# A fused two-layer decoder trunk: the last expert's end regrouped (picked rows, spread, last norm, branch order)

## The reference, cut to what matters

```
logits = xt @ w_router
top_v, top_i = top_k(logits, 2)
gates = softmax of the two, scattered to 8 experts
for e in range(8):
    h = xt @ w_gu[e]                                  # (256, 1024) @ (1024, 5632)
    y = (silu(h[:, :2816]) * h[:, 2816:]) @ w_down[e]
    out = out + gates[:, e] * y
x = layer_norm(alpha * x + out, g, b)                 # fp32, mean and variance over 1024
```

## Time and profile before

| | |
|---|---|
| median of 3 runs | 1303.49 us (1302.29 to 1306.15) |
| the profiled execution | 1302.73 us, of it the span 1300.9 us |
| TensorE busy | 1257.2 us (97%) |
| VectorE busy | 989.1 us (76%) |
| ScalarE busy | 823.9 us (63%) |
| GpSimd busy | 95.7 us (7%) |
| moved by transfers | 375.80 MB, mean 289 GB/s |

### The profile page before, as it was taken

The page is one execution under the profiler, slowest core; times in us unless marked ns, Lnnn a source line. Parts: engine busy times, 40 slices in busy tenths (PEclk is TensorE's granted clock), DMA queues, the critical chain, the costliest instruction groups (busy, mean ns, idle before and its releaser), DMA issues.

```text
span 1300.9 us, 17514 instructions
## 1 busy us (share of the span) xinstructions
PE 1257.2 (97%) x7133; PEld 1092.7 (84%) x7133; DVE 989.1 (76%) x827; ACT 823.9 (63%) x820; POOL 95.7 (7%) x116
## 2 busy tenths in 40 slices
PE   8999999999999979999999999999999999999994
PEld 8997987999988967888888888888888888888883
DVE  6876844554445575788888888888898988898896
ACT  5794343434434464577777777777777777778772
POOL 4043210200000100300000000000000000001000
PEclk9999998999999999999999999999999999999997
DMA  9743011997554522699999999999999999999990
GB/s 317 256 146 130 1 34 65 384 371 249 188 188 144 193 65 98 218 384 406 389 385 400 383 388 375 388 384 375 386 388 372 390 379 383 384 386 362 388 395 38
DMA packets 188854, 375.80 MB, mean 289 GB/s; under 512 B 12240, under 2 KB 69696, under 8 KB 188768
## 3 DMA queue, kind: packets, MB, share of 16 engines
q1 hardware_dynamic: 179744, 345.02, 73.3%
q0 software_dynamic: 6864, 25.81, 5.2%
q10 hardware_dynamic: 2160, 3.79, 0.8%
HBM read 354.12 MB, written 20.45 MB: 288 GB/s over the span
## 4 chain that ended last, share of the span: by engine, by line
PE 87%; DVE 5%; ACT 4%; DMA 2%; issue 1%; POOL 1%; SPq 1%; DVEq 0%; ACTq 0%
PE ps L1394 84%; PE ps L1791 1%; DMA raw<-in_moe_w_gu 1%; DVE lo L901 1%; DVE conv L982 1%; ACT hi L546 1%; DMA raw<-in_dn_w_in 1%; ACT sS L750 1%; PE ps L1784 0%; SPq L293 0%; DVE x L1360 0%; ACT ps L561 0%; ACT ps L599 0%; PE ps L1692 0%; ACT zn L599 0%
## 5 line engine op out<-in xcount | busy, mean ns | idle before, releaser
L901 DVE TENSOR_TENSOR lo<-raw,hi 128x2048 fp32r<-128x2048 f32 x326 | 744.8, 2297 | 173.6 <-ACT hi L546 172.7
L546 ACT ACTIVATE hi<-raw 128x2048 fp32r<-128x2048 f32 x326 | 625.4, 1919 | 317.1 <-PE ps L1394 287.3
L1394 PE MATMUL ps<-hi,xg_hi 128*128 128x512 f32 x704 | 277.5, 394 | 0.4 <-DVE lo L901 0.4
L1394 PE MATMUL ps<-hi,xg_lo 128*128 128x512 f32 x704 | 274.5, 390 | 0.0
L1394 PE MATMUL ps<-lo,xg_hi 128*128 128x512 f32 x704 | 274.1, 389 | 0.0
L1394 PE MATMUL ps<-xT_hi,hi 128*128 128x256 f32 x624 | 177.6, 285 | 2.1 <-DVE xT_lo L909 2.1
L1394 PE MATMUL ps<-xT_lo,hi 128*128 128x256 f32 x624 | 176.5, 283 | 0.0
L1394 PE MATMUL ps<-xT_hi,lo 128*128 128x256 f32 x624 | 176.5, 283 | 0.0
L1394 PEld LDWEIGHTS ps<-hi,xg_hi 128*128 128x128 f32 x704 | 132.2, 188 | 28.2 <-DVE lo L901 1.2
L1394 PEld LDWEIGHTS ps<-hi,xg_lo 128*128 128x128 f32 x704 | 132.1, 188 | 28.0
L1394 PEld LDWEIGHTS ps<-lo,xg_hi 128*128 128x128 f32 x704 | 132.3, 188 | 26.4
(11 more groups left out here) (293 smaller groups left out, 1266.5 us busy)
## 6 DMA issues: line engine op xcount, KB each, us to landing
raw<-in_moe_w_gu SPq DMA_DIRECT2D x352, 512.0 KB, 7.3
raw<-in_moe_w_down SPq DMA_DIRECT2D x176, 512.0 KB, 6.7
raw<-in_ffn_w_gu SPq DMA_DIRECT2D x44, 512.0 KB, 8.3
raw<-in_dn_w_in SPq DMA_DIRECT2D x32, 512.0 KB, 9.0
raw<-in_ffn_w_down SPq DMA_DIRECT2D x22, 512.0 KB, 4.0
xe<-xTf POOLq DMA_DIRECT2D x1, 8192.0 KB, 29.0
raw<-in_dn_w_out SPq DMA_DIRECT2D x8, 512.0 KB, 3.9
ys<-xTf POOLq DMA_DIRECT2D x1, 4096.0 KB, 40.1
```

The source lines that it names most:

```text
L546: act.activation(slot(hi, j), slot(raw, j), ACT.Copy).then_inc(hi_ready, 1)
L901: dve.tensor_tensor(slot(lo, j), slot(raw, j), slot(hi, j).bitcast(F32), ALU.subtract).then_inc(lo_ready, 1)
L1394: return pe.matmul(dst, lhsT, rhs, start=start, stop=stop)
```

## The change

Picked rows: the two rows of block 0 are added at units 26 and 28 of the last expert, the two of block 1 at unit 30. The spread goes half by half (columns 0 to 511 of both blocks, then the rest), with a signal for each of the four, and VectorE adds it in four operations of 512 columns with a sum each; `whole_sum` adds a block's two sums. The norm of block 0 begins (mean) ahead of block 1's second half. TensorE runs nine fillers behind the last unit, and the five ahead of the first expert are gone. SyncE branches first and waits for the stores behind the branch.

```
+        lnhalf = sb("lnhalf", [P, NB, 2])
...
-            sp_.wait_ge(out_done, 16 * NB)
             with sp_.If(full > P):
+                sp_.wait_ge(out_done, 16 * NB)
                 experts(1)
                 store(4)
                 sp_.wait_ge(out_done, 32 * NB)
+            sp_.wait_ge(out_done, 16 * NB)
...
-            def norm(i, bank, last=None):
+            def norm(i, bank, last=None, summed=None, between=None):
...
-                    mean(0)
-                    mean(1)
+                    for b in range(NB):
+                        if b and between:
+                            between()
+                        if summed:
+                            summed(b)
+                        mean(b)
                     centre(0)
                     centre(1)
                     finish(0)
...
+                            if p == 0 and last and b == 1 and l in (GU_E + 4, GU_E + 6):
+                                add_picked(0, (l - GU_E - 4) // 2)
                             if p == 0 and last and b == 1 and l == PER_E - 3:
-                                for n_ in range(2 * NB):
-                                    add_picked(n_ // 2, n_ % 2)
+                                add_picked(1, 0)
+                                add_picked(1, 1)
...
-            for b in range(NB):
-                dve.wait_ge(spread, b + 1)
-                dve.scalar_tensor_tensor(out=x[:, b, :], in0=ps[:, 2 * b:2 * b + 2, :].rearrange("p i n -> p (i n)"),
-                                         scalar=g7[:, b, :], in1=x[:, b, :], op0=ALU.mult, op1=ALU.add,
-                                         accum_out=lnsum[:, b:b + 1]).then_inc(spread_added, 1)
-            dve.wait_ge(spread_added, 2)
-            norm(3, None)
+            def add_spread(n_, b, i):
+                dve.wait_ge(spread, n_)
+                c = slice(512 * i, 512 * i + 512)
+                dve.scalar_tensor_tensor(out=x[:, b, c], in0=ps[:, 2 * b + i, :], scalar=g7[:, b, :], in1=x[:, b, c],
+                                         op0=ALU.mult, op1=ALU.add, accum_out=lnhalf[:, b, i:i + 1]).then_inc(spread_added, 1)
+
+            def whole_sum(b):
+                dve.wait_ge(spread_added, 3 + b)
+                step(dve.tensor_tensor(lnsum[:, b:b + 1], lnhalf[:, b, 0:1], lnhalf[:, b, 1:2], ALU.add))
+
+            add_spread(1, 0, 0)
+            add_spread(2, 1, 0)
+            add_spread(3, 0, 1)
+            norm(3, None, None, whole_sum, lambda: add_spread(4, 1, 1))
...
-            busy(5, 3)
...
-            for b in range(NB):
-                for i in range(2):
-                    pe.wait_ge(y_lo_here, i + 1)
+            busy(9, 7)
+            for i in range(2):
+                pe.wait_ge(y_lo_here, i + 1)
+                for b in range(NB):
                     mm(ps[:, 2 * b + i, :], onehT[:, b, :], y_hi[:, i, :], True, False)
-                    last = mm(ps[:, 2 * b + i, :], onehT[:, b, :], y_lo[:, i, :], False, True)
-                last.then_inc(spread, 1)
+                    mm(ps[:, 2 * b + i, :], onehT[:, b, :], y_lo[:, i, :], False, True).then_inc(spread, 1)
             with pe.If(full > P):
-                pe.wait_ge(spread_added, 2)
+                pe.wait_ge(spread_added, 4)
```

## The result

The changed kernel is slower. Its median is 1318.59 us (1317.43 to 1319.86, 4 runs), beside 1302.89 us (1302.24 to 1306.15, 4 runs) for the kernel before on the same chip: a ratio of 1.0106 on record, 95% interval 1.0089 to 1.0123 (the two medians alone divide to 1.0120). All four of its runs lie above all of before's. The forecast was 1299.3, the upper end of its range 1301.8. The profiled execution took 1317.43, its span is 1315.7.

What follows compares the result with a forecast made beforehand. TensorE's matmuls were taken to bound the kernel, with only the last 20.1 us open to the change. Gains of 2.45 (last norm) and 1.75 (branch) summed to 4.2 us: 1299.3 us, range 1297.5 to 1301.8.

Steps and rivals of the forecast that it cites:

- The step that failed: Start of the prediction, first to last expert: matmuls stand end to end, 2.72 us a unit, their number untouched by the diff.
- Picks (+0.30 on the PE): Last expert's units: picked adds between VectorE's cuts make unit 32 wait for its cut, 0.30 us more on TensorE.
- the upper bound: Last expert's units: the picked adds cost TensorE 0.6 us if unit 30 slips as well.
- y, earlier: Behind the last unit: the first half of y_lo starts at 1281.5, not 1283.03, and is done at 1282.2.
- Fillers (2.0 us, clock kept): Before the spread: nine fillers take 2.0 us, release the spread instead of y_lo, and keep the clock at 2.4 GHz.
- Halved adds, 0.70: Behind the spread: each 512-wide add takes 0.70 us, bounds 0.60 and 0.87; block 0's square at 1286.15, against 1289.01.
- What is late next: Last norm: the bound passes from GpSimd's power to VectorE's centres with 0.4 us to spare; gain 2.45 us.
- F': Forecast end of the last norm's finishes, 1292.35, against 1294.82 before.
- Branch: SyncE at the end: the taken jump costs 2.7 us and now overlaps the stores; gain 1.75 us.
- Rival A: SyncE's end: the 2.45 us behind the branch are the end of the stores, not the jump; 1301.0 us, chance 0.12.
- Five fillers at the start: zero: First expert: the 1.0 us saved turns into two pauses, 0.8 and 0.3; zero gain, bounds -1.0 and +1.7.
- rival C: First experts: without the five fillers pauses halve the clock, each unit passing on 2.4 us; four give 1308.9; chance 0.06.

Runs made afterwards that it cites:

- the direct comparison: Changed kernel with lnhalf declared last, SyncE's branch put back behind its wait for the stores: 1302.83 us; last stretch 18.02 us instead of 16.22.

## Why the prediction was wrong

**The step that failed** is the first: "one unit of the weight stream (12 matmuls of 512 columns) each 2.72 us, and nothing that the diff touches changes their number." Their number didn't change, their duration did. I took 2.72 us, so 227 ns a matmul, for a property of the shape; it is one of the shape and of two addresses, and the diff's first line moves one of the two. That line appears in no part of the sum. It costs 17 to 18.7 us: by 0.26 us for each of 66 stretches 17.2, by whole experts 18.4; the unused tensor alone made the experts 17.1 longer, and taking it out of the way gave back 17.0. Neither the forecast nor a rival had such a case: they argued about the last 20 us and the first four units, and took the 750 us between them as given. The 530 us ahead of the experts were taken as given too; there the changed kernel came out even (0.4 late), 2.6 ahead by its 256-column products and whatever else moved, and 3.1 lost with 10.2 us more of half clock.

**The rest, with the layout held equal.** The forecast gain was 4.2, the measured one 3.65 (1.7 parts in a thousand to 3.9, so 2.2 to 5.1 us). By landmarks in one execution each:

- *Picks (+0.30 on the PE).* Right. Unit 32's first matmul starts 0.2 late on the fresh cut and its second 0.1 more; unit 30, which the upper bound named, loses 0.1 as well. Together 0.3 to 0.4.
- *y, earlier.* Right: y_lo starts 0.70 after the last matmul's start (1283.10 to 1283.80), where 0.83 was forecast and 2.66 was before; the idle 0.94 ahead of it is still there, as in the earlier trace rows.
- *Fillers (2.0 us, clock kept).* Sizes right (2.17 with the last one's end), and wrong in worth: the clock held without them, and they cost 0.7. The prediction saw that they, not y_lo, release the spread, and didn't ask what a pause of 1.1 would do. That its total comes out near all the same hides this.
- *Halved adds, 0.70.* They are 0.68 apart (1286.00 to 1286.68). The square follows the last matmul's start by 5.42, where 5.48 was forecast. The page that spoke against halves ("VectorE: DVE Perf Modes" of the Trainium skill, TRN2 errata; its fixed 120 cycles from PSUM, an estimate of 0.125 us for each added operation) is borne out in direction: four take 2.7 against 2.6.
- *What is late next.* Right: the finish waits for VectorE, not for GpSimd. From the last matmul's start to F' it takes 11.72 us, against 14.45 before: 2.73, where 2.45 plus the 0.30 of delay, 2.75, was forecast. The halves, which the change gives most of its lines, are worth 0.15 when undone alone, the picks 1.24. The other 1.3 fit the spread at full clock (eight matmuls 0.23 apart, not 0.43 as in the earlier trace rows: 1.6); no run took that away alone, so this share is argued, not shown.
- *Branch.* Right: 2.75 us of jump against 2.7, from F' to the end 4.50 against 4.35, gain 1.60 (1.8 in the direct comparison) against 1.75. Rival A is out: beside the stores the jump costs no less.
- *Five fillers at the start: zero.* Right. The first product comes 1.1 sooner after the gather (3.60 for 4.71), and the experts take 1.7 longer, of which 0.3 to 0.4 is the picks' delay: the two cancel to 0.2. The pause before the third unit is there, with the clock at 1.00 behind it, so rival C is out too:

```profile
540.60 0.50 PE L1409 MATMUL ps<-hi,xg_hi 128*128 128x512 f32 x1 [0.74 <-DVE lo L903]
```

**What stays open.** Why the distance matters isn't shown, only that it does, in TensorE alone, with period 256. The stretch of half clock near 480 us varies: it was 3.4 us long in the kernel before and 10.2 in the one with everything moved by 256, which took 2.8 us longer from the attention to the experts (90.1 for 87.4), so 1.4 us for each 3.4. That may be why single runs of the kernel before scatter from 1302 to 1309; it isn't shown. Parts worth under 2 us were therefore read from the last stretch, in one execution each, not from the medians.

## What to carry to other kernels

Where an engine is 97% busy with one instruction, the first question to a diff is what could change that instruction's duration, declarations included: compare the start addresses of all operands before and after, and put new small tensors last. Read the pace as a count in a fixed window or as start to start, before and after, ahead of any reading of waits. And when one part of a change shortens a pause, ask again whether the other, which was to bridge it, is still wanted.

## What the hardware showed that was not expected

- The start-to-start time of back-to-back fp32r matmuls depends on the distance of their operands' start addresses modulo 256 bytes: 226.7 to 233.9 ns at 512 columns, 113.9 to 120.0 at 256. The best distance for 512 columns (0) is the slowest for 256, with 160 next to it at 119.8. Moving both by the same 32 bytes changes nothing (0.9996).
- An unused tensor of 16 bytes made a kernel of 1305.55 us slower by 1.25%.
- Pauses of TensorE of 1.08 us at the end and 0.74 us in the third unit left the granted clock at 1.00; behind one of 1.8 us in the gate and up, and behind one of 3.0 at the end, it stood at 0.50.
- A taken branch costs 2.75 us on SyncE with two stores on their way and 2.45 with none.
